# Fourier mixing: the feature transform forms the even and the odd part once, and VectorE writes their difference forwards and their sum backwards

## What is computed

```python
def fourier_mix(u):
    B, S, _ = u.shape
    ug = u.astype(jnp.float32).reshape(B, S, F_GROUPS, F_GROUP_DIM)
    y = jnp.fft.fft2(ug, axes=(1, 3), norm='ortho').real
    return y.reshape(B, S, F_WIDTH).astype(u.dtype)

def token_mix(h, w_in, w_fourier, w_ret, w_out):
    proj = h @ w_in
    u_f, q, k, v, g, a_f, a_r = jnp.split(proj, offsets, axis=-1)
    y_f = fourier_mix(u_f) @ w_fourier
    y_r = retention_branch(q, k, v, g) @ w_ret
    merged = jax.nn.sigmoid(a_f) * y_f + jax.nn.sigmoid(a_r) * y_r
    return merged @ w_out
```

## Time and profile before

| | |
|---|---|
| median of 3 runs | 2137.96 us |
| the profiled execution | 2141.47 us |
| its span, first to last instruction | 2139.7 us |
| TensorE busy | 2107.8 us (99%) |
| VectorE busy | 1491.6 us (70%) |
| ScalarE busy | 985.9 us (46%) |
| GpSimd busy | 378.1 us (18%) |
| mean granted TensorE clock | 0.992 of full speed |

### The profile page before, as it was taken

How to read it: one execution, slowest core, us unless ns; L and a number is a source line. 1 busy time by engine, 2 the same in 40 slices (tenths; PEclk the granted TensorE clock), 3 DMA queues, 4 the chain that set the end, 5 groups by cost and what they waited for, 6 DMA issues and landing times.

```text
span 2139.7 us, 36520 instructions
## 1 busy us (share of the span) xinstructions
PE 2107.8 (99%) x14084; PEld 1926.4 (90%) x14084; DVE 1491.6 (70%) x2149; ACT 985.9 (46%) x1455; POOL 378.1 (18%) x262
## 2 busy tenths in 40 slices
PE   8999999999999999999999999999999999999998
PEld 7999999999999999999877888888888888899998
DVE  5766888976766899967988534798433376866454
ACT  3444456644444556644245533432243245755453
POOL 0330302310510213202301012120020021121020
PEclk8999999999999999999999999999999999999999
DMA  7775667786665666672554323266633244664553
GB/s 282 279 265 197 232 222 243 245 287 205 220 236 179 223 198 210 197 246 85 183 174 158 101 89 104 94 198 222 196 108 99 86 145 157 204 214 161 179 186 99
DMA packets 109592, 396.34 MB, mean 185 GB/s; under 512 B 12408, under 2 KB 13056, under 8 KB 109056
## 3 DMA queue, kind: packets, MB, share of 16 engines
q1 hardware_dynamic: 108160, 389.99, 54.2%
q0 software_dynamic: 1280, 4.20, 0.6%
HBM read 393.09 MB, written 1.05 MB: 184 GB/s over the span
## 4 chain that ended last, share of the span: by engine, by line
PE 89%; DVE 7%; ACT 2%; DMA 2%; issue 1%; POOL 0%; SPq 0%; DVEq 0%; ACTq 0%; POOLq 0%
PE bank L492 23%; PE bank L493 23%; PE bank L494 23%; DVE w_lo L1382 3%; PE bank L545 2%; PE bank L546 2%; PE bank L547 2%; PE bank L625 1%; PE bank L628 1%; DMA stage<-in_stream 1%; PE bank L572 1%; DVE stage L1403 1%; PE bank L584 1%; PE bank L859 1%; PE bank L906 1%
## 5 line engine op out<-in xcount | busy, mean ns | idle before, releaser
L1382 DVE TENSOR_TENSOR w_lo<-stage,w_hi 128x1024 fp32r<-128x1024 f32 x536 | 696.1, 1312 | 497.4 <-ACT w_hi L981 496.6
L981 ACT ACTIVATE w_hi<-stage 128x1024 fp32r<-128x1024 f32 x536 | 566.2, 1059 | 886.5 <-PE bank L494 650.2
L492 PE MATMUL bank<-h_hi,w_hi 128*128 128x256 f32 (+1 forms) x2592 | 800.6, 309 | 8.5 <-DVE w_lo L1382 5.9
L493 PE MATMUL bank<-h_lo,w_hi 128*128 128x256 f32 (+1 forms) x2592 | 794.6, 307 | 0.0
L494 PE MATMUL bank<-h_hi,w_lo 128*128 128x256 f32 (+1 forms) x2592 | 794.5, 307 | 0.0
L492 PEld LDWEIGHTS bank<-h_hi,w_hi 128*128 128x128 f32 x2592 | 494.9, 191 | 39.9 <-DVE w_lo L1382 9.9
L493 PEld LDWEIGHTS bank<-h_lo,w_hi 128*128 128x128 f32 x2592 | 495.0, 191 | 23.0 <-issue 0.7
L494 PEld LDWEIGHTS bank<-h_hi,w_lo 128*128 128x128 f32 x2592 | 494.9, 191 | 22.6
L1403 DVE SCALAR_TENSOR_TENSOR stage<-stage,cvec 128x1024 f32<-128x1024 f32 x188 | 255.5, 1360 | 5.6 <-DMA stage<-in_stream 3.3
L492 PE MATMUL bank<-f_hi,w_hi 128*128 128x512 f32 (+1 forms) x512 | 172.5, 337 | 0.0
L494 PE MATMUL bank<-f_hi,w_lo 128*128 128x512 f32 (+1 forms) x512 | 172.0, 336 | 0.0
(11 more groups left out here) (239 smaller groups left out, 3011.0 us busy)
## 6 DMA issues: line engine op xcount, KB each, us to landing
stage<-in_stream SPq DMA_DIRECT2D x728, 512.0 KB, 4.3
bias<-in_bias POOLq DMA_DIRECT2D x16, 256.0 KB, 3.1
X<-in_x SPq DMA_DIRECT2D x2, 1024.0 KB, 6.8
cvec<-in_cvec SPq DMA_DIRECT2D x3, 512.0 KB, 5.0
decay<-in_decay SPq DMA_DIRECT2D x1, 1024.0 KB, 5.4
out<-X SPq DMA_DIRECT2D x4, 256.0 KB, 2.1
rope<-in_rope SPq DMA_DIRECT2D x2, 256.0 KB, 5.2
wsgu<-in_wsgu SPq DMA_DIRECT2D x2, 256.0 KB
```

The source lines that it names most:

```text
L492: mm(out, w_hi[:, slot, w], xh[:, c, 0:T], start=first, stop=False)
L493: mm(out, w_hi[:, slot, w], xl[:, c, 0:T], start=False, stop=False)
L981: A(w_hi[:, m % NR, :], stage[:, n % NS, :], ACT.Copy).then_inc(hi_ready, 1)
L1382: do(V.tensor_tensor(w_lo[:, m % NR, :], stage[:, n % NS, :], w_hi[:, m % NR, :].bitcast(F32), ALU.subtract), unit_done, done_value(n))
```

## The change

TensorE leaves the even part (cos*A, 129 columns) and the odd part (sin*B, 127 columns) of each chunk side by side in the bank. ScalarE copies the whole bank to a new SBUF tile `yo`, and the two columns that need no partner (0 and 128) to a second new tile `yf`. VectorE writes even - odd forwards and even + odd backwards into `yf`, with the even part read from PSUM and the odd from `yo`; this frees the bank. ScalarE rounds `yf` to `h_hi`, and VectorE writes yf - h_hi to `h_lo`. `yo` and `yf` have two buffers each, so the copies of bank cc wait for the h_lo of cc - 2.

```diff
@@ tiles
+        yo = sb("yo", [P, 2, 2, S], F32, ph + 40 * KB)
+        yf = sb("yf", [P, 2, 2, S], F32, ph + 44 * KB)
-        dftg = sb("dftg", [P, 3, P], F32, ph + 66 * KB)
+        dftg = sb("dftg", [P, 2, P], F32, ph + 66 * KB)
@@ TensorE
-                        mm(out[:, a:a + P], dftg[:, 0, :], AB[:, c, 0:P], start=True, stop=False)
-                        mm(out[:, a + 1:a + P], dftg[:, 1, :], AB[:, c, P + 1:S], start=False, stop=True)
-                        mm(out[:, a + P:a + S], dftg[:, 0, :], AB[:, c, P:0:-1], start=True, stop=False)
-                        last = mm(out[:, a + P + 1:a + S], dftg[:, 2, :], AB[:, c, S - 1:P:-1], start=False, stop=True)
+                        mm(out[:, a:a + P + 1], dftg[:, 0, :], AB[:, c, 0:P + 1], start=True, stop=True)
+                        last = mm(out[:, a + P + 1:a + S], dftg[:, 1, :], AB[:, c, P + 1:S], start=True, stop=True)
                 def fourier_ready(i):
-                    wait_taken(pe, grp(L, "F2", i))
+                    pe.wait_ge(s["f_ready"], 4 * L + i + 1)
@@ ScalarE
+                def fourier_hi(cc):
+                    wait_taken(act, grp(L, "F2", cc))
+                    A(h_hi[:, 2 * cc:2 * cc + 2, S:T2], yf[:, cc % 2, :, :], ACT.Copy).then_inc(s["fhi_ready"], 1)
                 for cc in range(DC // 2):
                     g = grp(L, "F2", cc)
                     wait_filled(act, g)
-                    A(h_hi[:, 2 * cc:2 * cc + 2, S:T2], bank_of(g)[:, :].rearrange("p (c t) -> p c t", c=2),
-                      ACT.Copy).then_inc(s["fhi_ready"], 1)
+                    b = bank_of(g)[:, :].rearrange("p (c t) -> p c t", c=2)
+                    if cc >= 2:
+                        act.wait_ge(s["f_ready"], 4 * L + cc - 1)
+                    A(yo[:, cc % 2, :, :], b, ACT.Copy).then_inc(s["yo_ready"], 1)
+                    A(yf[:, cc % 2, :, 0:P + 1:P], b[:, :, 0:P + 1:P], ACT.Copy).then_inc(s["yo_ready"], 1)
+                    if cc:
+                        fourier_hi(cc - 1)
+                fourier_hi(DC // 2 - 1)
@@ VectorE
+                def unfold(cc):
+                    g = grp(L, "F2", cc)
+                    dve.wait_ge(s["yo_ready"], 8 * L + 2 * cc + 2)
+                    b = bank_of(g)[:, :].rearrange("p (c t) -> p c t", c=2)
+                    even, odd = b[:, :, 1:P], yo[:, cc % 2, :, P + 1:S]
+                    do(V.tensor_tensor(yf[:, cc % 2, :, 1:P], even, odd, ALU.subtract))
+                    take(V.tensor_tensor(yf[:, cc % 2, :, S - 1:P:-1], even, odd, ALU.add), g)
+
+                def fourier_lo(cc):
+                    dve.wait_ge(s["fhi_ready"], 4 * L + cc + 1)
+                    do(V.tensor_tensor(h_lo[:, 2 * cc:2 * cc + 2, S:T2], yf[:, cc % 2, :, :],
+                                       h_hi[:, 2 * cc:2 * cc + 2, S:T2].bitcast(F32), ALU.subtract), s["f_ready"], 4 * L + cc + 1)
                 for cc in range(DC // 2):
-                    g = grp(L, "F2", cc)
-                    dve.wait_ge(s["fhi_ready"], 4 * L + cc + 1)
-                    take(V.tensor_tensor(h_lo[:, 2 * cc:2 * cc + 2, S:T2], bank_of(g)[:, :].rearrange("p (c t) -> p c t", c=2),
-                                         h_hi[:, 2 * cc:2 * cc + 2, S:T2].bitcast(F32), ALU.subtract), g)
+                    unfold(cc)
+                    if cc:
+                        fourier_lo(cc - 1)
+                fourier_lo(DC // 2 - 1)
@@ the tables
-    dftg = np.stack([np.cos(a), -np.sin(a), np.sin(a)], axis=1)
+    dftg = np.stack([np.cos(a), np.sin(a)], axis=1)
```

More of the change, by code:

```diff
@@ L320, in program @@
             "c_ready", "const_ready", "sq_ready", "sq_used", "sq_added", "std_ready",
-            "t_ready", "hhi_ready", "h_ready", "xf_ready", "uq_rot", "uk_rot", "fhi_ready", "g_sig", "sq2_ready",
+            "t_ready", "hhi_ready", "h_ready", "xf_ready", "f_ready", "yo_ready", "uq_rot", "uk_rot", "fhi_ready", "g_sig", "sq2_ready",
             "rstd2_ready", "yn_ready", "rhi_ready", "r_ready", "m_ready", "mhi_ready", "mm_ready", "lin_ready",
```

## The result

The changed kernel takes 2142.71 us (median of 9 runs, 2140.70 to 2145.46), the kernel before beside it 2137.70 (9 runs, 2135.64 to 2140.87). The ratio is 1.0025, 95% interval 1.0014 to 1.0035: slower by 5.3 us, between 3.0 and 7.5. The forecast of +6.0 us and 2144.0 stands 1.3 us above the median.

What follows compares the result with a forecast made beforehand. TensorE, busy 99% of the span, was taken as the bound: -7.06 us of matmuls, +5.5 and +4.6 of waits, +3.0 of clock give +6.0, 2144.0 us on the median; range 2138 to 2149, the forecast's own 2141 to 2147.

Steps and rivals of the forecast that it cites:

- F2: TensorE at F2: two matmuls per chunk in place of four save 3.53 us a layer, 7.06 us in all.
- The h_lo take turns with GpSimd: VectorE on F2: each h_lo, reading two SBUF tiles, waits for GpSimd's k rotation, 2.86 us a turn.
- Rival 2: The h_lo are not held by GpSimd; shorter TensorE waits leave -3.4 us, 2134.5 us; chance 0.08.
- The small prices: ScalarE and VectorE on F2: 0.2 us per 4-column copy, 0.416 per 254-number instruction, nothing for writing backwards, 0.60 for h_hi.
- The waits: TensorE idles for v1_0's w_lo 5.5 us in layer 0, 4.6 in layer 1, starting it 1.95 and 1.05 us later.
- The clock: Behind each new TensorE wait at v1_0 the granted clock falls: 0 to 2.4 us, taken as 1.5, +3.0 for two.
- the idle time that ends at 26.77: Earlier TensorE idle time: clock stayed at 0.50 until 31.6 at least, about 2.4 us lost, the upper price of a wait.
- the idle time at 65.50: Earlier TensorE idle time of 1.88 us: clock 0.50 for 3.4 us behind it, 1.7 us lost.
- The sum: Whole kernel: saved matmuls, two waits and the clock make +6.0 us, 2144.0 us on the median, 0.28% slower.
- Rival 1: The waits at v1_0 come but the clock does not fall behind them: +3.0, 2141.0 us; chance 0.13.
- Rival 3: All the saving arrives at v1_0 and v1_1 if VectorE adds less than 1.3 us: -7.06, 2130.9 us; chance 0.03.
- Rival 4: Clock costs 2.4 us at each wait and a later short idle time costs 1.7: +9.5, 2147.5 us; chance 0.10.

Runs made afterwards that it cites:

- e2: The changed kernel without GpSimd's rotation of k (left out of the computation): 9.0 us faster than the kernel before.
- e8: Sum and difference in the PSUM bank as in e1, modulation units moved behind v1_2, in both layers: 2129.07 us, 0.9958 of the kernel before.
- e1: The changed kernel, but VectorE writes sum and difference back into the PSUM bank, without yf and the small copies: 3.0 us faster than the kernel before.
- e3: The kernel before with its own matmuls, but ScalarE copies each bank to SBUF and h_lo reads that copy: 3.2 us slower than the kernel before.
- e6: The changed kernel with GpSimd rotating k in two halves, the first as soon as k0 is there: 8.1 us slower than the kernel before.
- e7: e1 with GpSimd rotating k in two halves as in e6: 1.1 us slower than the kernel before.
- e9: The changed kernel, yf still in SBUF, with the modulation units moved as in e8: 5.8 us slower than the kernel before.
- e4: The kernel before with F2's two matmuls per chunk, sum and difference left out of the computation: 4.7 us faster than the kernel before.
- e5: The changed kernel with 20 matmuls of no use put ahead of v1 in both layers: 3.0 us slower than the kernel before.

## Why the prediction was right

- **F2**: 3.53 us a layer predicted, 3.57 seen (e2, e8).
- **The h_lo take turns with GpSimd**: right in mechanism and size. Turns of 2.86 predicted, 2.8 to 2.9 measured; e1 and e2 took the hold away in two ways, e3 made it alone. Rival 2 (not held) falls.
- **The small prices** (0.2 for 4 columns, 0.42 for 254 numbers, nothing for writing backwards): 0.17 to 0.19, 0.41, and the backwards one (L1588) took 0.41 like its forward twin. In e1 it wrote the bank backwards in 0.42 (L1586). The h_hi from SBUF, left at 0.60, took 0.63 to 0.64.
- **The waits**: 5.5 and 4.6 predicted, 5.27 and 4.36 idle measured; counted as the prediction counts them, from when v1_0 was wanted to its start, 5.4 and 4.5. Their net cost without the clock, +1.95 and +1.05, came out as +2.02 and +1.10 in e3.
- **The clock**: right in kind; the size holds over many runs, and single executions lie on or above it. I took 1.5 us a wait. The stretch less 28.26 less the wait gives 36.35 - 28.26 - 5.27 = 2.8 in either layer, 1.8 and 1.9 in the second profile; together with e6, e7 and e9, 1.8 to 2.9 over nine waits. About 0.3 of each is not the clock's, since a wait costs that beyond its idle time at 2.4 GHz too (e3: 33.85 - 31.83 - 1.71 = 0.31; e1 and e4 give the same for each wait). What is left is 2.5 a wait in the first profile, 1.5 and 1.6 in the second, and 2.1 in the mean of the nine. Over many runs e5, where the clock stayed up, lies 2.3 and 3.0 us below the changed kernel, for both waits together, where I had put 3.0. That 1.5 was a choice between 0 and 2.4 from three rows, and a single profile could have answered it with 2.5; so its coming out is in part luck.
- **A row of the clock read too strongly**: behind the idle time that ends at 26.77 the clock was low, and I took this for the price of that wait. But in the kernel before the granted clock is 0.50 from 15 to 20 us too, with TensorE busy throughout, and in 22 to 26. The row shows what a low clock costs, not that this wait brought it down. Only the idle time at 65.50 shows a fall behind a wait.
- **The sum**: by stretches +8.1 and +6.2 in two profiles where +6.0 was forecast; over many runs +5.3 and +6.0. That the runs show somewhat less than the stretches of the first profile is not explained; the scatter of the clock's price covers it, but wasn't followed through all runs.
- **The rivals**: 0.57 stood on within 0.3%, and 0.25% was measured. Rival 1 (clock stays) falls with the windows. Rival 2 (h_lo not held) was priced well: e1 makes its case, with -2.8 in the stretches and -3.0 measured where -3.4 was worked out. Rival 3's condition was too weak: VectorE was to add less than 1.3 us at v1_0 and v1_1; in e4 it adds nothing, and TensorE waits at v1_2 and v1_1 all the same. Rival 4's later loss was not seen: TensorE's other waits for w_lo are 7.5 and 7.0 us where they were 6.6 and 6.8.

## What to carry to other kernels

Before moving a result of PSUM into SBUF, ask what GpSimd does in those us: the same subtraction took 0.68 us from a bank and 2.8 from a tile, and unfolding in place, with the modulation units moved away from the units split right behind it, turned +5.3 us into -9.0. Count such a hold by GpSimd's instructions, one for each VectorE instruction that reads two tiles, and look in VectorE's queue for what can stand behind the critical split. Price a new wait of TensorE with the clock behind it, and if the wait can't be removed, compare it with one filled by idle matmuls.

## What the runs showed of the hardware

- All nine waits at v1 of 3.5 us or more were followed by a granted clock of 0.50, in two of them only within 1 us behind the restart, and each cost another 1.8 to 2.9 us, of which 0.3 comes with every wait; none of those at v1 of up to 1.9 us was. Yet one of 1.88 us elsewhere was the earlier trace rows, and one of 1.87 us at v1 (e7) was not, so the length of the wait alone doesn't tell.
- Cutting GpSimd's instructions in half made each turn shorter and all of them together longer (e6, +8.1 us): 1.28 us of work took about 2.2 in turns, and there were twelve.
- A w_lo pending through a whole turn of GpSimd took 3.35 to 3.43 us (e4 and e8), as against 1.98 and 2.05 in the earlier trace rows. The first of the three in e8, put down while a GpSimd instruction was running, took 2.22 us beside the same work, so a short hold in a profile doesn't mean a cheap one for the next instruction in the queue.
